# Two transformer blocks on one core: the first mixer's second gates as 512-column products over two banks, another order of the first down projection's weights, and four banks in the last branches

## The reference

```python
# first block
xn = _rmsnorm(x, mix_norm[l])
h = xn @ w_in[l]
lru_x, lru_gate, q, k, v, qi, ki, wi, gate_a, gate_b = _split_cols(h)
ya = _rg_lru(...); ya = (ya * jax.nn.gelu(lru_gate)) @ w_lru_br[l]
yb = _dsa_attention(...) @ w_attn_br[l]
merged = jax.nn.sigmoid(gate_a) * ya + jax.nn.sigmoid(gate_b) * yb
x = x + merged @ w_out[l]
up = _rmsnorm(x, ffn_norm[l]) @ w_up[l]
g_ffn = _causal_dwconv(up[..., :D_FF], ffn_conv_w[l], ffn_conv_b[l])
x = x + (jax.nn.gelu(g_ffn) * up[..., D_FF:]) @ w_down[l]          # D_FF = 3072
# second block
x = x + 0.5 * swiglu_ffn(rms_norm(x, g1), ...)
proj = rms_norm(x, mix_norm) @ w_mix_in
merged = g_a * (y_a @ w_branch_a) + g_b * (y_b @ w_branch_b)       # y_a, y_b: two attentions
x = x + merged @ w_o
x = rms_norm(x + 0.5 * swiglu_ffn(rms_norm(x, g2), ...), final_norm)
```

## Time and profile before

| | |
|---|---|
| median of 3 runs | 1052.1 us |
| the profiled execution | 1051.96 us, span 1050.2 us |
| TensorE busy | 1037.2 us (99%) |
| VectorE, ScalarE, GpSimd busy | 776.7 us (74%), 588.9 us (56%), 183.8 us (18%) |
| mean DMA rate | 178 GB/s |
| mean granted clock of TensorE | 0.998 |

### The profile page before, as it was taken

The page is one execution under the profiler, slowest core; times in us unless marked ns, Lnnn a source line. Parts: engine busy times, 40 slices in busy tenths (PEclk is TensorE's granted clock), DMA queues, the critical chain, the costliest instruction groups (busy, mean ns, idle before and its releaser), DMA issues.

```text
span 1050.2 us, 18083 instructions
## 1 busy us (share of the span) xinstructions
PE 1037.2 (99%) x6894; PEld 948.7 (90%) x6894; DVE 776.7 (74%) x962; ACT 588.9 (56%) x831; POOL 183.8 (18%) x209
## 2 busy tenths in 40 slices
PE   8999999999999999999999999999999999999998
PEld 7899999899888887899888888999989998888887
DVE  5799875768999996558887866575686688878653
ACT  5665799445656555457545444446576455454442
POOL 0400001222311211012222221010000222222210
PEclk9999999999999999999999999999999999999999
DMA  7745366755766666466776576664434557765761
GB/s 232 243 148 159 121 203 198 241 161 162 198 172 188 187 178 196 120 204 195 204 199 185 140 215 181 201 200 160 160 122 161 161 161 201 197 180 143 218 183 41
DMA packets 289762, 186.94 MB, mean 178 GB/s; under 512 B 6719, under 2 KB 286342, under 8 KB 289702
## 3 DMA queue, kind: packets, MB, share of 16 engines
q1 hardware_dynamic: 289006, 184.97, 59.9%
q10 hardware_dynamic: 696, 1.14, 0.3%
HBM read 184.94 MB, written 1.08 MB: 177 GB/s over the span
## 4 chain that ended last, share of the span: by engine, by line
PE 83%; DVE 10%; ACT 3%; issue 3%; DVEq 0%; DMA 0%; ACTq 0%; POOL 0%; POOLq 0%
PE psum L1886 19%; PE psum L1922 18%; PE psum L2391 10%; PE psum L1891 10%; PE psum L2394 5%; DVE wl L1260 5%; PE psum L2443 3%; PE psum L1861 2%; PE psum L1863 2%; PE psum L1862 2%; DVE logit L1693 2%; PE psum L2446 1%; DVE page_x L1664 1%; ACT logit L979 1%; DVE page_x L1676 1%
## 5 line engine op out<-in xcount | busy, mean ns | idle before, releaser
L1260 DVE TENSOR_TENSOR wl<-raw,wh 128x2048 fp32r<-128x2048 f32 (+3 forms) x210 | 414.0, 1988 | 95.1 <-ACT wh L591 94.8
L591 ACT ACTIVATE wh<-raw 128x2048 fp32r<-128x2048 f32 (+3 forms) x211 | 329.9, 1582 | 26.2 <-PE psum L1863 11.9
L1886 PE MATMUL psum<-parts,wh 128*128 128x512 f32 x1226 | 294.1, 391 | 0.0
L1886 PEld LDWEIGHTS psum<-parts,wh 128*128 128x128 f32 x1226 | 224.9, 188 | 43.8 <-DVE wl L1260 0.5
L1922 PE MATMUL psum<-parts,wh 128*128 128x256 f32 x1120 | 203.3, 285 | 1.9 <-issue 1.1
L1922 PEld LDWEIGHTS psum<-parts,wh 128*128 128x128 f32 x1120 | 173.9, 192 | 3.6 <-issue 2.1
L1891 PEld LDWEIGHTS psum<-parts,wl 128*128 128x128 f32 x1226 | 158.0, 191 | 6.5
L1891 PE MATMUL psum<-parts,wl 128*128 128x256 f32 x1226 | 160.0, 283 | 0.0
L1922 PE MATMUL psum<-parts,wl 128*128 128x256 f32 x560 | 156.0, 283 | 0.0
L2391 PE MATMUL psum<-parts,wh 128*128 128x512 f32 x476 | 121.0, 394 | 2.6 <-POOL parts L1200 2.6
L957 ACT ACTIVATE page_q<-psum 128x512 f32<-128x512 f32 x68 | 40.4, 594 | 125.2 <-PE psum L1891 125.0
(11 more groups left out here) (267 smaller groups left out, 1223.5 us busy)
## 6 DMA issues: line engine op xcount, KB each, us to landing
raw<-in_ffn_w_in SPq DMA_DIRECT2D x88, 512.0 KB
raw<-in_w_up SPq DMA_DIRECT2D x48, 512.0 KB
raw<-in_w_in SPq DMA_DIRECT2D x23, 1024.0 KB
raw<-in_w_mix_in SPq DMA_DIRECT2D x20, 1024.0 KB
raw<-in_ffn_w_out SPq DMA_DIRECT2D x32, 448.0 KB
raw<-in_w_down SPq DMA_DIRECT2D x24, 512.0 KB
raw<-in_ffn_w_out SPq DMA_DIRECT2D x16, 512.0 KB
raw<-in_w_attn_br SPq DMA_DIRECT2D x4, 1024.0 KB
```

The lines of the kernel that those rows point to most:

```text
L591: act.activation(place(wh, u), place(raw, u), ACT.Copy).then_inc(rounded, 1)
L1260: dve.tensor_tensor(place(wl, u), place(raw, u), place(wh, u).bitcast(F32), ALU.subtract).then_inc(rest, 1)
L1886: mm(banks[base + s], wh[:, u % RING, w:w + P], both[:, t0 + k, :, :].rearrange("p h t -> p (h t)"), start=(k == 0), stop=False)
```

## The change

- DOWN_ORDER: in DN1 the pieces go (0,0), (0,1), (1,0), (1,1), (0,2), (1,2), then chunks 2 to 7 as before. Loads, rounding, rests and products all follow this list. DN2 and DN3 keep theirs.
- The GB units go through both_halves over banks 5/6, 1/2, 3/4, 5/6 (GATE_BASE). ScalarE copies the low part to logit (gb_low), VectorE adds (gb_sum, gb_added), ScalarE takes Tanh in place (gb_tanh). The branches' banks shift by one place, and branch units 0 to 2 wait for gb_added.
- POOL_LOWS[0]: 5 to 2. Six lows of the first norm are VectorE's, two GpSimd's.
- Start: all four transfers of x on SP; round_unit(2) between the squares and rest_unit(2) ahead of the norm's steps; copy_x ahead of the key step; spread_inv between the halves of unit 2; round_unit(3) ahead of copy_inv(0).
- MIX2: values (O) go with the next even unit, ahead of its turns (T), on TensorE and ScalarE.
- BA and BB rotate over banks 0 to 3, with bank_free to match.

```diff
+DOWN_ORDER = {"DN1": [(0, 0), (0, 1), (1, 0), (1, 1), (0, 2), (1, 2)] + [(c, r) for c in range(2, 8) for r in range(3)]}
...
-POOL_LOWS = {0: 5, 2: 3, 4: 5}
+POOL_LOWS = {0: 2, 2: 3, 4: 5}
...
-for _e, _work in {6: dict(S=6), 8: dict(S=8, T=6), 9: dict(O=6), 10: dict(S=10, T=8), 11: dict(O=8), 12: dict(S=12, T=10),
-                  13: dict(O=10), 14: dict(S=14, T=12), 15: dict(O=12), 16: dict(S=16, T=13), 17: dict(O=13),
-                  18: dict(T=14), 19: dict(O=14)}.items():
+for _e, _work in {6: dict(S=6), 8: dict(S=8, T=6), 10: dict(S=10, T=8, O=6), 12: dict(S=12, T=10, O=8),
+                  14: dict(S=14, T=12, O=10), 16: dict(S=16, T=13, O=12), 18: dict(T=14, O=13), 19: dict(O=14)}.items():
...
+                if g >= group(U["BA"]):
+                    return banks[(g - group(U["BA"])) % 4]
...
-        BRANCH_BASE = (3, 5, 1, 3, 5, 1, 3)
+        GATE_BASE, BRANCH_BASE = (5, 1, 3, 5), (1, 3, 5, 1, 3, 5, 1)
...
             square_tokens(0)
+            round_unit(2)
             square_tokens(1)
             act.wait_ge(stat_done, 1)
             act.activation(rms[:, :], msq[:, 0, :], ACT.Sqrt, bias=eps[:, :], scale=1.0 / D).then_inc(root_done, 1)
-            round_unit(2)
+            round_unit(3)
             copy_inv(0)
-            round_unit(3)
...
+            def gb_tanh(m):
+                act.wait_ge(gb_added, m + 1)
+                part = gate_b[:, 2 * m:2 * m + 2, :]
+                act.activation(part, part, ACT.Tanh, scale=0.5).then_inc(read_a, 1)
             for m in range(4):
                 if m:
                     round_unit(25 + m)
-                if m == 0:
-                    act.wait_ge(lru_ix, 2)
-                evac(group(U["GB"] + m), gate_b[:, 2 * m:2 * m + 2, :], func=ACT.Tanh, scale=0.5)
+                group_done(group(U["GB"]) + m)
+                act.activation(logit[:, m, :].rearrange("p (a t) -> p a t", a=2), low_part(GATE_BASE[m]), ACT.Copy).then_inc(gb_low, 1)
+                if m:
+                    gb_tanh(m - 1)
                 if m == 1:
                     lru_root(1)
             y_high(1)
+            gb_tanh(3)
...
+            rest_unit(2)
             dve.wait_ge(sq_done, 2)
             dve.tensor_tensor(msq[:, 0, :], msq[:, 0, :], msq[:, 1, :], ALU.add).then_inc(stat_done, 1)
             norm_inverse(0)
-            rest_unit(2)
+            for e in range(4):
+                copy_x(e)
...
             lru_input(1, 25)
+            dve.wait_ge(lru_ix, 2)
             rest_unit(26)
+            gb_sum(0)
             rest_unit(27)
+            gb_sum(1)
             lru_scan(1)
+            gb_sum(2)
             lru_output(1)
             rest_unit(28)
+            gb_sum(3)
...
-            spread_inv(0)
             half_pair(1, 1, (2,), **raw_parts).then_inc(mm_done, 1)
-            pair(2, parts=unscaled(0))
+            pair(2, parts=unscaled(0), between=lambda: spread_inv(0))
...
-            for u in range(23, U["YB"]):
-                pair(u)
+            for m in range(4):
+                unit_ready(U["GB"] + m)
+                if m == 0:
+                    pe.wait_ge(ol_done, 6)
+                elif m == 1:
+                    pe.wait_ge(read_a, READ_BY["A"][group(U["RI1"]) + 4])
+                elif m == 3:
+                    pe.wait_ge(gb_added, 1)
+                both_halves(U["GB"] + m, GATE_BASE[m], xx).then_inc(mm_done, 1)
...
-                if n == 2:
-                    pe.wait_ge(read_a, READ_BY["A"][group(U["GB"] + 3) + 1])
-                elif n > 2:
+                if n < 3:
+                    pe.wait_ge(gb_added, n + 2)
+                else:
                     pe.wait_ge(read_d, READ_BY["D"][group(U["YB"]) + n - 2])
...
+                if "O" in MIX2[e]:
+                    values(MIX2[e]["O"])
                 if "T" in MIX2[e]:
                     for t in tiles_turned(MIX2[e]["T"]):
                         turn(t)
-                if "O" in MIX2[e]:
-                    values(MIX2[e]["O"])
```

More of the change, by code:

```diff
@@ L1106, in _ @@
                     act.activation(ob_raw(t), o_bank[:, 0:w], ACT.Copy).then_inc(ob_copied, 1)
+                if "T" in MIX2[e]:
+                    for t in tiles_turned(MIX2[e]["T"]):
+                        copy_turned(t)
                 if "S" in MIX2[e]:
@@ L1337, in _ @@
             dve.tensor_tensor(by_half(widx), backwards(bank(0)[64:72, 0:T]), backwards(root[64:72, :]), ALU.mult).then_inc(read_d, 1)
-            for e in range(4):
-                copy_x(e)
             rest_unit(3)
@@ L2331, in branch_unit @@
                 ins.then_inc(mm_done, 1)
-            pe.wait_ge(ol_done, 6)
             for n in range(4):
@@ L2372, in ffn_down @@
                 hidden = parts[:, HIDDEN["UP" + name[2]]:H1 + K, :, :]
-                def one(c):
-                    ps = banks[down_base(name, c)]
-                    pe.wait_ge(read_d, READ_BY["D"][g0] + c - 2)
-                    k0 = 0
-                    for r, nk in enumerate(pieces):
-                        u = u0 + 3 * c + r
-                        unit_ready(u)
-                        w0 = half(u) * SLOT // 2
-                        if c == 0 and r < 2:
-                            pe.wait_ge(lo_done, lows + k0 + nk)
-                        for k in range(nk) if c == 7 else ():
-                            first, last = k0 + k == 0, k0 + k == sum(pieces) - 1
-                            ins = three(ps[:, 0:T], u % RING, w0 + k * P, hidden[:, k0 + k, 0, :], hidden[:, k0 + k, 1, :], first, last)
-                        for ks in (range(nk),) if c < 7 else ():
-                            for k in ks:
-                                if c == 0 and r == 2:
-                                    pe.wait_ge(lo_done, lows + k0 + k + 1)
-                                mm(ps, wh[:, u % RING, w0 + k * P:w0 + k * P + P],
-                                   hidden[:, k0 + k, :, :].rearrange("p h t -> p (h t)"), start=(k0 + k == 0), stop=False)
-                            for k in ks:
-                                ins = mm(ps[:, 0:T], wl[:, u % RING, w0 + k * P:w0 + k * P + P], hidden[:, k0 + k, 0, :],
-                                         start=False, stop=(k0 + k == sum(pieces) - 1))
-                        ins.then_inc(mm_done, 1)
-                        k0 += nk
@@ L2398, in ffn_down @@
-                for c in range(8):
-                    one(c)
+                for j, (c, r) in enumerate(DOWN_ORDER[name]):
+                    u, nk, k0 = u0 + j, pieces[r], sum(pieces[:r])
+                    ps, w0 = banks[down_base(name, c)], half(u) * SLOT // 2
+                    if r == 0:
+                        pe.wait_ge(read_d, READ_BY["D"][g0] + c - 2)
+                    unit_ready(u)
+                    if c == 0 and r < 2:
+                        pe.wait_ge(lo_done, lows + k0 + nk)
+                    if c == 7:
+                        for k in range(nk):
+                            ins = three(ps[:, 0:T], u % RING, w0 + k * P, hidden[:, k0 + k, 0, :], hidden[:, k0 + k, 1, :],
+                                        k0 + k == 0, k0 + k == sum(pieces) - 1)
+                    else:
+                        for k in range(nk):
+                            if c == 0 and r == 2:
+                                pe.wait_ge(lo_done, lows + k0 + k + 1)
+                            mm(ps, wh[:, u % RING, w0 + k * P:w0 + k * P + P],
+                               hidden[:, k0 + k, :, :].rearrange("p h t -> p (h t)"), start=(k0 + k == 0), stop=False)
+                        for k in range(nk):
+                            ins = mm(ps[:, 0:T], wl[:, u % RING, w0 + k * P:w0 + k * P + P], hidden[:, k0 + k, 0, :],
+                                     start=False, stop=(k0 + k == sum(pieces) - 1))
+                    ins.then_inc(mm_done, 1)
```

38 lines of the change are left out of this document (21 added, 17 removed).

## The result

The changed kernel takes 1057.04 us in the median of five runs (1056.12 to 1057.42), the kernel before 1052.1 beside it: ratio 1.0049, 95% interval 1.0038 to 1.0060, so it is slower by 5.2 us. 1054.8 was forecast, in a range up to 1057.2; the ratio gives 1057.3, just beyond its end. The profiled execution took 1057.36 for a span of 1055.5 us, 5.3 more than before.

What follows compares the result with a forecast made beforehand. TensorE, busy 99% of the span, was taken as the bound. Start -1.5, GB +3.0, DN1 +1.4 and second mixer -0.2 sum to +2.7 on 1051.96, giving 1054.7; with 0.1 for the median, 1054.8 us, range 1051.0 to 1057.2.

Steps and rivals of the forecast that it cites:

- The second mixer: Second mixer's new order of values and turns: -0.2 us, ends 0 and -1.2.
- five interruptions of units become none: Second mixer: all work stays, five interruptions of units vanish; -1.2 us end is five times 0.23.
- DN1: New piece order: GpSimd wait passed, 3.6 us hole before the fourth piece, clock falls; +1.4 us, ends 0.0 and +1.8.
- At 0.50 for 3 us, 1.5 us of work is lost: Clock fall behind DN1's 3.6 us hole: 3 us at granted clock 0.50, costing 1.5 us of work.
- The start: Up to GB: x arrives sooner, unit 2 starts earlier, hole of 1.07 us shrinks; -1.5 us, ends -1.0 and -2.2.
- GB: Gate units as 512-column products: saves 0.8 us but waits 1.5 and 2.1 us; +3.0 us net, ends +2.3 and +3.6.
- Rival A: Clock also falls in GB, behind its two holes: another 1.6 us, 1056.4 us; chance 0.2.
- Four banks: Last branches rotating over four banks: the only wait there is for VectorE's `parts`; 0.0 us.
- B: Rival: the clock doesn't fall in DN1; 1053.4 us, chance 0.14.
- C: Rival: start gives -3.3 us, if unit 2 starts at 17.4 and the whole 1.07 us hole goes; 1053.0 us, chance 0.11.
- D: Rival: DN1 gives back all 4.3 us, needing the fourth unit's rest by 395.3; 1049.1 us, chance 0.06.
- E: Rival: GB's order doesn't cause the delay, as ScalarE could pass its Tanh by; no size or own chance given.

Runs made afterwards that it cites:

- changed, again: The changed kernel measured once more, nothing altered, against the kernel before; ratio 1.0049, +5.2 us.
- combined kernel: Changed kernel with the second mixer as before and earlier roundings and rests in GB and DN1; 1044.54 us, ratio 0.9934 to the kernel before.
- one step back: Kernel before with the second mixer's new table and order, but the values of step 10 back behind unit 13; ratio 1.0008, +0.7 us.
- DN1 alone, filled: Kernel before with DN1's new order and 28 unread products where TensorE stood before the fourth piece; ratio 0.9998, -0.2 us.
- down_early2: Kernel before with DN1's new order, and rounding and rests for the fourth, fifth and seventh pieces moved earlier; ratio 0.9955, -4.7 us.

## Why the prediction was right and wrong

Slower was forecast and slower it is, by 5.3 us in the profiles against a forecast of 2.7. Two steps failed, each by more than a microsecond, and the start took 0.6 back.

**The second mixer, wrong in sign.** -0.2 forecast, +1.1 in the profile, +1.3 alone. The step that failed is "five interruptions of units become none". The interruptions were counted as cost; one of them, the values between units 13 and 14, was also what TensorE did while VectorE emptied the bank that unit 14's second half needs. Put back, it takes 0.9 of the 1.1 us away. The prediction asked what is queued behind the moved step on ScalarE, not who comes sooner on TensorE. With +1.1 in this term the forecast would have been 1056.1.

**DN1, right alone and too small in the whole kernel.** +1.4 forecast, +1.6 by the run alone, +3.1 in the changed kernel's profile. The step that failed there is "At 0.50 for 3 us, 1.5 us of work is lost". The hole (3.52 for 3.6), its cause, the late seventh piece (0.94 for 0.9) and the fall were right, but one row showed one fall, and I took its length for a property of the place. From the fourth piece's start to the seventh's it takes 9.59 us without a fall (changed, again), 11.13 with one of 3.4 us (DN1 alone) and 12.23 with one of 6.8 (changed): 1.5 and 2.6 us lost. Time from DN1's start to its seventh piece, from the timelines of all profiled executions but the combined kernel's, which is as the last row:

| execution | wait before the slow stretch | clock at 0.50 | to the seventh piece |
|---|---|---|---|
| old order: before | 1.36 + 1.26 | 3.4 us | 21.27 |
| old order: start alone | 1.39 + 1.26 | 3.4 us | 21.26 |
| old order: second mixer alone | 1.36 + 1.26 | 3.4 us | 21.63 |
| old order: one step back | 1.37 + 1.27, then 0.42 | 3.4 us | 22.15 |
| old order: GB, three roundings early | 1.41 + 1.26, then 0.43 | 3.4 us | 22.21 |
| old order: GB, two roundings early | 1.41 + 1.26, then 0.42 | none | 20.63 |
| old order: GB alone | 1.41 + 1.26 | 6.8 us | 22.76 |
| new order: changed, again | 3.51 | none | 21.64 |
| new order: DN1 alone | 3.54 | 3.4 us | 23.21 |
| new order: changed | 3.52 | 6.8 us | 24.29 |
| new order: DN1 alone, filled | 0.18 | none | 21.68 |
| new order: fourth and seventh unit early | 1.86 | none | 18.88 |
| new order: fourth, fifth and seventh early | none | none | 16.76 |

The old order has a fall of its own, and not always the same. Held against an old execution with a fall of the same length the new order costs 1.0 us (none), 1.0 to 2.0 (3.4 us) and 1.5 (6.8 us); held against the one profile of the kernel before, +0.4, +1.9 or +3.0. A single +1.4 with ends 0 and +1.8 couldn't hold that. Of the 2.6 us that the profile lies above the forecast, 1.7 are here.

**The start, too small in the profile.** -1.5 forecast, its end -2.2; -2.1 in the profile, -1.6 by the run alone, -1.9 over the profiled starts. The order of events was the one described. Unit 2 ended 1.0 us ahead where 1.3 was forecast, and of the hole nothing is left where 0.1 to 0.8 was. Since four of ten executions with the old start don't have that hole, the 1.07 us of the earlier trace rows was in part luck of the one execution that was read.

**GB, right.** +3.0 forecast, +3.1 read at branch unit 1, +3.2 up to DN1 and by the run alone. The two holes of 1.5 and 2.1 us were 1.81 and, without a fall, 1.61. The step that carried it was laying both engines' orders out in series with durations of rows. Rival A's mechanism took place in both profiles of the changed kernel, and its price was wrong: 1.6 us was added to the sum, though the fall began before a hole of 2.1 us that could take it. With a fall branch unit 1 starts 31.66 us behind the first GB unit, without it, in GB alone, 31.67.

**Four banks, right.** 27.47 and 27.48 us.

**The rivals.** B's condition, no fall in DN1, was met in the second profile of the changed kernel, which is 2.7 us shorter than the first. Of C's two conditions one came, the hole went whole, and the other didn't: unit 2 started at 18.43, not at 17.4. D didn't come, as argued: the fourth unit's rest was late by the table load, and down_early2 shows that this unit, the fifth and the seventh were all that stood against it. E was excluded rightly.

## What to carry to other kernels

When an order is changed so that a wait is passed, lay out all units that follow, not the next one: here each mended hole came back one unit later until every rounding had moved. A step that seems to interrupt TensorE may be the cover under which another engine empties its bank; ask who arrives sooner once it is gone. Price a hole of a few microseconds on TensorE as the hole plus a fall of the clock that may come or not and may be twice as long as the one in the profile, unless another wait behind it takes the fall up. Before a hole or a fall in one profile becomes a term of a sum, see whether other executions of the same code have it: the hole at the start was missing in four of ten.
